# First mixer of a two-layer block: where modulation chunks 12 to 15 are summed, and when the scan's powers and between-states are made

## The reference, cut to what matters

```python
mod = sc @ ada_w[li] + ada_b[li]                       # 6 * 1024 columns a layer
sh1, sc1, g1, sh2, sc2, g2 = jnp.split(mod[:, None, :], 6, axis=-1)
...
p = softmax(q @ k.T * scale);  attn = p @ v            # first mixer, one half
states = s5_scan(ul, lam_bar, b_bar, ctx_final)        # s[t] = lam * s[t-1] + b u[t]
y = y + einsum('blgp,ghp->blgh', states, c_mat).real
z = gelu(y); s5 = z * sigmoid(z @ glu_w + glu_b)       # first mixer, other half
x = x + g1 * (concat([attn, s5]) @ w_out)
x = x + g2 * moe(modulate(rmsnorm(x), sh2, sc2), ...)
```

## Time and profile before

| what | value |
|---|---|
| median of 3 runs | 1443.02 us (1441.14 to 1443.29) |
| the profiled execution's own time | 1447.34 us |
| its span | 1445.5 us |
| busy: PE, DVE, ACT, POOL | 1303.6, 639.0, 300.4, 60.2 us |
| HBM | 347 GB/s over the span |
| granted TensorE clock, mean | 0.967 |

### The profile page before, as it was taken

The page is one execution under the profiler, slowest core; times in us unless marked ns, Lnnn a source line. Parts: engine busy times, 40 slices in busy tenths (PEclk is TensorE's granted clock), DMA queues, the critical chain, the costliest instruction groups (busy, mean ns, idle before and its releaser), DMA issues.

```text
span 1445.5 us, 21852 instructions
## 1 busy us (share of the span) xinstructions
PE 1303.6 (90%) x9044; PEld 678.7 (47%) x9044; DVE 639.0 (44%) x1175; ACT 300.4 (21%) x508; POOL 60.2 (4%) x112
## 2 busy tenths in 40 slices
PE   5999888999999978889888999999999978888888
PEld 1445335764444433334345676874454434333334
DVE  5998862254433222232233678864433323222232
ACT  2226342311111111111112113131111111111111
POOL 0000680000000000000000000000000000000000
PEclk9999999899999999999999999999999999999999
DMA  9673874959999999999998772587999999999995
GB/s 374 244 200 83 164 240 183 412 226 371 421 425 420 426 430 429 427 430 427 427 422 294 292 284 117 206 361 303 374 426 421 422 430 425 429 428 427 428 425 241
DMA packets 52598, 502.76 MB, mean 348 GB/s; under 512 B 9548, under 2 KB 16460, under 8 KB 20044
## 3 DMA queue, kind: packets, MB, share of 16 engines
q1 hardware_dynamic: 51948, 499.18, 86.0%
q10 hardware_dynamic: 544, 2.10, 0.4%
HBM read 496.57 MB, written 4.69 MB: 347 GB/s over the span
## 4 chain that ended last, share of the span: by engine, by line
PE 59%; DMA 28%; DVE 8%; issue 2%; SPq 1%; ACT 1%; DVEq 0%; ACTq 0%
PE ps L752 55%; DMA arena<-in_w_experts 23%; DMA arena<-in_ada_w 4%; PE ps L1070 2%; PE ps L446 2%; SPq L490 1%; DVE arena L2049 1%; ACT arena L1416 1%; DVE arena L2150 0%; DVE arena L1876 0%; PE ps L805 0%; DVE arena L1871 0%; DVE arena L1872 0%; DVE arena L1889 0%; PE ps L1017 0%
## 5 line engine op out<-in xcount | busy, mean ns | idle before, releaser
L752 PE MATMUL ps<-arena 128*32 128x512 f32 (+10 forms) x8224 | 1219.9, 485 | 122.0 <-issue 48.6
L752 PEld LDWEIGHTS ps<-arena 128*32 128x32 f32 (+5 forms) x8224 | 616.9, 130 | 709.9 <-issue 586.9
L1416 ACT ACTIVATE arena<-ps 128x512 f32<-128x512 f32 (+6 forms) x305 | 168.5, 552 | 926.2 <-PE ps L752 767.5
L1416 ACT ACTIVATE arena<-arena 128x256 f32<-128x256 f32 (+7 forms) x143 | 94.5, 682 | 153.2 <-DVE arena L2110 58.3
L2090 DVE SCALAR_TENSOR_TENSOR arena<-arena,ps 128x256 f32<-128x256 f32 x44 | 21.1, 480 | 233.7 <-ACT arena L1416 233.7
L2108 DVE CAST arena<-ps 128x512 bf16<-128x512 f32 x42 | 29.1, 692 | 165.2 <-PE ps L752 165.2
L2045 DVE COPY arena<-ps 128x512 f32<-128x512 f32 x44 | 30.4, 692 | 126.9 <-PE ps L752 126.9
L2078 DVE TENSOR_TENSOR arena<-arena 128x1024 bf16<-128x1024 f32 x42 | 51.5, 1225 | 37.3 <-ACT arena L1416 37.0
L1070 PE MATMUL ps<-arena 128*128 128x128 f32 x352 | 52.8, 273 | 0.0
L2110 DVE TENSOR_TENSOR arena<-ps,arena 128x1024 f32<-128x1024 f32 x42 | 51.4, 1224 | 1.4
L742 POOL MEMSET arena<- 128x1 f32 x2 | 0.2, 102 | 1192.3 <-PE ps L1070 1192.3
(11 more groups left out here) (234 smaller groups left out, 481.1 us busy)
## 6 DMA issues: line engine op xcount, KB each, us to landing
arena<-in_w_experts SPq DMA_DIRECT2D x76, 3072.0 KB, 20.8
arena<-in_w_experts SPq DMA_DIRECT2D x80, 1024.0 KB, 11.6
arena<-in_w_experts SPq DMA_DIRECT2D x38, 2048.0 KB, 19.8
arena<-in_ada_w SPq DMA_DIRECT2D x40, 1024.0 KB, 6.6
arena<-in_hy_w_in SPq DMA_DIRECT2D x6, 2048.0 KB, 11.1
arena<-in_ada_w SPq DMA_DIRECT2D x4, 2048.0 KB, 22.9
arena<-in_w_shared SPq DMA_DIRECT2D x2, 3072.0 KB, 10.1
arena<-in_hy_w_out SPq DMA_DIRECT2D x1, 4096.0 KB, 12.1
```

Of the source, the lines that this page charges most:

```text
L752: return pe.matmul(out, lhsT, rhs, start=start, stop=stop, skip_group_check=skip)
L1416: return act.activation(out, in_, func, **kw)
```

## The change

Four things are done.

1. On TensorE only chunk 11 stays in the softmax loop, now in step 2, ahead of that step's wait. Chunks 12 to 15 are summed on VectorE (`half_sum`, the body of `modulation_sum` made a function), four instructions a half. The first half of chunk 12 comes behind the softmax list and ahead of the last `attend_out`; then its second half, chunks 13 and 14, and the first half of chunk 15, all ahead of the wait for `y_mm`; the last half behind the eviction of y. TensorE folds the four sums with four products behind the gate products, and `ada_turn` goes behind part 7.
2. SP's list: chunk 12, the two attention loads, chunk 13, the wait for the last `attend`, `glu_w`, chunks 14 and 15, `w_s5`. The loads are as large as before and the buffer is the same; a half of the buffer now comes free when VectorE has summed it.
3. GpSimd squares all four powers when `qh_normed` is 1, into buffers of their own, and not between the levels of its tree.
4. The states between are made in iteration 14 of VectorE's softmax list, which there waits for `scan_done` 1.

```diff
-            for i in range(FILL_AT + 1, LATER - 1):
-                ada_load(i)
+            ada_load(FILL_AT + 1)
             load(w_att[0], A["ev_w_out"][:, 0:1], "wout_in")
             load(w_att[1], A["ev_w_out"][:, 1:4], "wout_in")
-            ada_load(LATER - 1)
+            ada_load(FILL_AT + 2)
             sp.wait_ge(sem("pv_mm"), HEADS // 2)
             sp.wait_ge(sem("wout_in"), 32)
             load(glu_w, A["glu_w"], "wout_in")
-            load(w_s5, A["ev_w_out"][:, 4:], "wout_in")
+            ada_load(FILL_AT + 3)
+            ada_load(LATER - 1)
+            load(w_s5, A["ev_w_out"][:, 4:], "w_s5_in")
...
+            pool.wait_ge(sem("qh_normed"), 1)
+            squared(pair_a, pair_b, A8, B8)
+            for n in range(3):
+                squared(*powers[n + 1], *powers[n])
             pool.wait_ge(sem("est_ready"), 8)
...
-                if n > 1:
-                    squared(step_a, step_b, a, b)
-                    a, b = step_a, step_b
...
             for n in range(2 * HEADS):
                 if n + 2 < 2 * HEADS:
                     scores(n + 2)
+                if n == 2:
+                    ada_chunk(pe, FILL_AT)
                 pe.wait_ge(sem("prob_ready"), n + 1)
...
-                if n % 3 == 0 and n > 0:
-                    ada_chunk(pe, FILL_AT + n // 3 - 1)
...
             attention_part(0)
-            ada_turn(pe, 0)
             attention_part(1)
...
+            pe.wait_ge(sem("ada_mm"), LATER)
+            for k in range(4):
+                a = 2 * (GROUP - 1 - (FILL_AT + 1 + k - FIRST))
+                last = pe.matmul(ps[32 * k:32 * k + 2 * GROUP, 7, :], first_pick[:, a:a + 2 * GROUP], first_sums[k], start=False, stop=k == 3, skip_group_check=True)
+            last.then_inc(sem("sums_mm"), 1)
             attention_part(7).then_inc(sem("att_mm"), 1)
+            ada_turn(pe, 0)
+            pe.wait_ge(sem("w_s5_in"), 16)
             pe.wait_ge(sem("s5_out"), 4)
...
             turned(act, f, ch, 2 * HEADS - 1)
-            ada_evict(act, f, ch, 0)
-            ada_copy(act, f, ch, 0)
...
+            ada_evict(act, f, ch, 0)
+            ada_copy(act, f, ch, 0)
...
+            def half_sum(i, half, out):
+
+                dve.wait_ge(sem(f"ada_in{half}"), 16 * (i - FIRST + 1))
+                for k in range(4):
+                    w, c = ada_half(i, half)[:, k], scz[:, 4 * half + k, 2 * GROUP - 2:2 * GROUP - 1]
+                    ins = ts(out, w, c, None, M) if half == 0 and k == 0 else stt(out, w, c, out, M, AD)
+                    if k < 3:
+                        ch(ins)
+                    elif half == 0:
+                        ins.then_inc(sem("ada_used"), 1)
+                        dve.wait_ge(sem("ada_used"), i - FIRST + 1)
+                    else:
+                        ins.then_inc(sem("ada_mm"), 1)
+                        dve.wait_ge(sem("ada_mm"), i + 1)
...
+                if n == 2 * HEADS - 2:
+                    dve.wait_ge(sem("scan_done"), 1)
+                    ch.then(pair_step(st[:, 3:2 + XCH:2], st[:, 2:2 + XCH:2], st[:, 2:2 + XCH:2, ::-1], est[:, XCH:NCH:2], XCH // 2), "combined")
                 if n >= 6 and n % 4 == 2:
                     attend_out(dve, ch, (n - 6) // 4)
...
+            half_sum(FILL_AT + 1, 0, first_sums[0])
             attend_out(dve, ch, HEADS // 2 - 1)
+            half_sum(FILL_AT + 1, 1, first_sums[0])
+            for half in range(2):
+                half_sum(FILL_AT + 2, half, first_sums[1])
+            for half in range(2):
+                half_sum(FILL_AT + 3, half, first_sums[2])
+            half_sum(FILL_AT + 4, 0, first_sums[3])
 
             dve.wait_ge(sem("y_mm"), 1)
             ch.then(dve.tensor_copy(ys.rearrange("p t (q b) c -> p b q t c", b=2)[:, 0],
                                     ps[:, 3, :].rearrange("p (q t c) -> p q t c", t=T5, c=C5)), "y_evicted")
+            half_sum(FILL_AT + 4, 1, first_sums[3])
```

More of the change, by code:

```diff
@@ L209, in program @@
         bm = at(rb, 4096).rearrange("p (b t r m) -> p b t r m", b=2, t=8, r=2)
-        step_a, step_b = (at(rb + 64 * i, 64).rearrange("p (r t) -> p r t", r=2) for i in (0, 1))
-        pair_a, pair_b = (at(rb + 64 * i, 64).rearrange("p (r t) -> p r t", r=2) for i in (2, 3))
-        tmp_a = at(rb + 256, 64).rearrange("p (r t) -> p r t", r=2)
+        powers = [[tiles(ri + 128 * i + 64 * j, 2, NT5) for j in (0, 1)] for i in range(4)]
+        pair_a, pair_b = powers[0]
+        tmp_a = tiles(ri + 512, 2, NT5)
         tree, pair_in, wide = (at(rb + 1024 * i, 1024).rearrange("p (s r t) -> p s r t", r=2, t=NT5) for i in (1, 2, 3))
@@ L421, in program @@
         row_pick = at(h3 + 18176, 4 * GROUP - 2)
+        first_sums = [at(rb + 1024 + ADC * k, ADC) for k in range(4)]
+        first_pick = at(rb, 4 * GROUP - 2)
         def short(c):
@@ L456, in ada_evict @@
         def ada_evict(act, f, ch, n):
-            act.wait_ge(sem("ada_mm"), (LATER, NADC)[n])
+            if n == 0:
+                act.wait_ge(sem("sums_mm"), 1)
+            else:
+                act.wait_ge(sem("ada_mm"), NADC)
             ch.then(f(adline[n], ps[:, 7, :], ACT.Copy), "adrow_ready")
@@ L706, in _ @@
             step(tree, a8, b8, est[:, 0:XCH:2], est[:, 0:XCH:2, ::-1], est[:, 1:XCH:2], wide, tree)
-            squared(pair_a, pair_b, A8, B8)
-            a, b, src, n = pair_a, pair_b, tree, 16
-            for out in (est[:, 0:8], tree[:, 0:4], est[:, 0:2], st[:, 2:3]):
+            src, n = tree, 16
+            for out, (a, b) in zip((est[:, 0:8], tree[:, 0:4], est[:, 0:2], st[:, 2:3]), powers):
                 n //= 2
@@ L1054, in _ @@
             pe.wait_ge(sem("z_ready"), 2)
-            pe.wait_ge(sem("wout_in"), 16 * 4)
+            pe.wait_ge(sem("wout_in"), 16 * 3)
             for j in range(4):
@@ L1907, in _ @@
                     ch(ins) if n == 2 else ch.then(ins, "combined")
+                if n == 2 * HEADS - 2:
+                    dve.wait_ge(sem("scan_done"), 1)
+                    ch.then(pair_step(st[:, 3:2 + XCH:2], st[:, 2:2 + XCH:2], st[:, 2:2 + XCH:2, ::-1], est[:, XCH:NCH:2], XCH // 2), "combined")
                 if n >= 6 and n % 4 == 2:
                     attend_out(dve, ch, (n - 6) // 4)
-            dve.wait_ge(sem("scan_done"), 1)
-            ch.then(pair_step(st[:, 3:2 + XCH:2], st[:, 2:2 + XCH:2], st[:, 2:2 + XCH:2, ::-1], est[:, XCH:NCH:2], XCH // 2), "combined")
+            ch(dve.memset(first_pick, 0.0))
+            ch(dve.memset(first_pick[:, 2 * GROUP - 2:2 * GROUP - 1], 1.0))
+            half_sum(FILL_AT + 1, 0, first_sums[0])
             attend_out(dve, ch, HEADS // 2 - 1)
+            half_sum(FILL_AT + 1, 1, first_sums[0])
[4 more added lines that the diff above has]
+            half_sum(FILL_AT + 4, 0, first_sums[3])
             dve.wait_ge(sem("y_mm"), 1)
@@ L2235, in modulation_sum @@
             def modulation_sum(n):
-                i = LATER + 2 * n
                 for half in range(2):
-                    dve.wait_ge(sem(f"ada_in{half}"), 16 * (i - FIRST + 1))
-                    for k in range(4):
-                        w, c = ada_half(i, half)[:, k], scz[:, 4 * half + k, 2 * GROUP - 2:2 * GROUP - 1]
-                        ins = ts(ada_sums[n], w, c, None, M) if half == 0 and k == 0 else stt(ada_sums[n], w, c, ada_sums[n], M, AD)
-                        if k < 3:
-                            ch(ins)
-                        elif half == 0:
-                            ins.then_inc(sem("ada_used"), 1)
-                            dve.wait_ge(sem("ada_used"), i - FIRST + 1)
-                        else:
-                            ins.then_inc(sem("ada_mm"), 1)
-                            dve.wait_ge(sem("ada_mm"), i + 1)
+                    half_sum(LATER + 2 * n, half, ada_sums[n])
             dve.wait_ge(sem("sc_ready"), 1)
```

1 line of the change is left out of this document (added).

## The result

The changed kernel takes 1448.35 us (median of 20 runs, 1444.18 to 1452.32), the kernel before 1443.03 us (20 runs): a ratio of 1.0029, 95% interval 1.0020 to 1.0037, so by the ratio 4.2 us slower (2.9 to 5.3; the two medians lie 5.3 apart). The forecast of "slower" and the range (1440.3 to 1450.0) hold, and 1446.1 us (+3.1) is near; of the terms behind that sum, several do not hold.

What follows compares the result with a forecast made beforehand. TensorE's products and the experts' weights were taken to bound the kernel, so only the first mixer's end counted. Terms 0.1 + 0.5 + 1.7 + 0.8 gave +3.1 us on 1443.02, 1446.1 us; range 1440.3 to 1450.0.

Steps and rivals of the forecast that it cites:

- Carrying one to one: End of the first mixer: whatever it loses or gains goes into the total one to one.
- Parts 1 and 2: Softmax loop and scan: chunk 11 costs nothing, two chunks leaving save 3.8 us; `scan_done` comes at 213.2, 6.2 earlier.
- the early squarings: nothing: GpSimd's squarings moved early, while VectorE reads mostly PSUM: no cost, at most their own 20 instructions of 0.3 us.
- Part 3: VectorE from iteration 14: stands for the scan until 213.3; `attend(3)` takes 2.85, its eviction done at 226.25, 3.2 us earlier.
- Part 4: VectorE's sums up to y: two loads in series at 5.1 us put y's eviction at 248.8, +0.1 us.
- rival B: Modulation loads take their middle 6.8 us: y evicted at 252.2, +3.4 on the sum, 1449.5 us; slower, chance 0.17.
- Part 5, fold, turn and clock: TensorE behind y: lower clock after idling +0.5 us, folding products and turn on the path +1.7.
- Part 5, the router's loads: Router's loads behind the experts' queue land 4.6 us later, needed 2.3 later: +0.8 us, between nothing and 2.
- small loads slip past: Lower bound at the router: its small loads are not held up by the queue, so their term is nothing.
- A: The sums keep pace: y evicted 4.3 to 8.9 earlier, total -1.6 to -6.2 us; faster, chance 0.25.
- C: Nothing reaches the end: router's loads slip past, clock does not fall, 1444.8 us; same, chance 0.12.

Runs made afterwards that it cites:

- f1: r6 with GpSimd's second tree level waiting until VectorE has done the rope's last 96x2048 product; ratio 0.9963 to the kernel before.
- e1: The changed kernel, but VectorE evicts y ahead of the first half of chunk 15, not behind it; ratio 1.0040 to the kernel before.
- e4: The changed kernel with a second buffer place for modulation chunks and `w_s5` loaded behind all sums; ratio 1.0032 to the kernel before.
- r0: The changed kernel with the router's three small loads issued ahead of expert 2; ratio 1.0032 to the kernel before.
- d8: The kernel before with eight unneeded products on TensorE behind part 7; ratio 1.0052, 7.5 us slower.
- r6: e4 with states between and last `attend_out` behind the softmax, ahead of all sums, and router's loads ahead of experts 1 and 2; 0.9949, 1435.8 us.
- rb: The kernel before with the router's loads issued ahead of expert 2, as control; ratio 0.9994.
- e3: The kernel before with only the early squarings on GpSimd and the states between in iteration 14, modulation chunks on TensorE; ratio 1.0007.

## Why the prediction came out right, point by point

The direction came out for the reason given, sums that wait for loads ahead of y. That +3.1 lies so near +4.2 is in good part luck. y was to be 0.1 late and was 5.2 late; fold, turn and clock came to 1.7 and not 2.2, the router's wait to 1.0 and not 0.8. Two things that the sum did not have took most of the excess back: the last 96 products took 1.16 less than in the trace of before, and the start of the second layer some 2.6 less (see "Carrying one to one").

**Parts 1 and 2 (right).** Chunk 11 cost nothing: it lies in a gap (181.00) that was there. The transposes of step 12 came at 209.62; counted from the softmax's start that is 34.3, against 36.9 before, so the two chunks won 2.6 of the 3.8. `scan_done` let VectorE go at 214.06, 0.8 after my 213.3.

**Part 2, "the early squarings: nothing" (failed step, +1.9 us on two products).** The squarings themselves were harmless, but taking them out of the tree brings GpSimd's 128x512 operations beside the rope's last two products, where the small squarings had stood. I had counted the moved instructions and not what moves up into their place. The second product took 3.24 to 3.26 us in every kernel with the early squarings except f1, and 2.29 in every one without them and in f1: 0.95 for certain, and in the changed kernel 0.9 more on the first one. The softmax starts 1.43 later and not 1.86, since the first product began 0.43 earlier in this trace (167.45 against 167.88). What this costs in the total is not shown: f1 takes it away and is no faster. Part 3 otherwise went as written: a wait of 2.84 in iteration 14 (4.6 predicted, since VectorE came later), the last scaling done at 222.09 (221.1), `attend(3)` in 3.68 us and not in 2.85. I had misread the latter as a time at half clock: it began at 226.08, behind the stretch at 0.50, and 226 to 230 was granted 0.76; in the changed kernel 224 to 228 was granted 0.52. Its eviction ended at 228.2, where I had 226.25.

**Part 4, "+0.1" (failed step: it measured +5.2).** The mechanism was the right one, loads in series in front of the eviction, but I had followed the wrong halves. By terms, the 5.1 between my 248.8 and the 253.90: 2.0 come from the late `attend(3)`; 0.35 from the wait for chunk 13's second half, whose load took 5.4; 0.65 more up to the end of chunk 14; and 2.1 from a third wait that I had not seen. I had let the first halves of chunks 14 and 15 be "landed meanwhile". But the load of 15's first half can be issued only when 14's first half has been summed, and that load took 8.5, not 5.1, with `glu_w` (1 MiB) issued 2.45 us before it on the same queue: landed at 242.8, summed at 245.7, and from there another 5.2 for the next. So the chain ran through the first halves, 8.5 + 5.2, and not through two second halves of 5.1 each. This is near rival B's price by another road: B had put y at 252.2. e1 and e4 show that the order and the places are the cause; no run has `glu_w` elsewhere. By an estimate from the same rows, with 5.4 for the load behind it too, y would have come at about 251.5.

The fit of the Trainium skill's page "DMA: Bandwidth & Descriptors", section "Anatomy of one DMA" (2.0 us plus bytes over 436 GB/s, an estimate of 4.4 for these loads), is for transfers issued by GpSimd and does not carry over to these: five loads of the changed kernel that had little in front of them took 5.0 to 5.8, and the one behind 1 MiB 8.5.

**Part 5, fold, turn and clock: +2.2 predicted, +1.70 measured.** The transposes of y behind 6.93 of idle took 1.97 where they took 1.03 before; at half the granted clock, as I had it from the earlier trace rows. The stretches of the changed kernel (columns as there):

```profile
250.00:254.00 4.00, 0.00 (x0) 0.00 (x0) 2.84 (x5) 0.00 (x0) 0.00 (x0) 0.72 1.03 363
254.00:258.00 4.00, 3.35 (x12) 3.09 (x13) 3.60 (x5) 1.26 (x2) 0.00 (x0) 0.50 1.02 434
```

TensorE idles in the first and is at 0.50, its lower level of 1.2 GHz, in the second. In e1, with 1.98 of idle, they took 1.09, and y to the last 96 was 14.99: so fold and turn are worth 0.7 on the path (1.6 from the start of the transposes to the last 96, 14.24 against 12.60, less the 0.9 by which the transposes follow y's eviction sooner, 0.75 against 1.66), and the clock about 1.0, where I had 1.7 and 0.5.

**Part 5, the router's loads: +0.8 (failed step).** In the changed kernel it was +1.03, near enough. But it was no small term: it is a second bound at almost the same height as the first, and I had given it 2 us at most. The case of my sum (y at 248.8) was nearly run: e1 has y at 248.12, and its router's products start 6.26 later than before, not 3.1. There the queue behind the modulation loads had not started at 246.0 but with `w_s5` at 248.48, since the last chunk's load came later; and `small loads slip past`, my lower bound, is refuted by 10.0 us for 256 KB. So one term was too low in each of two lanes that run side by side: what counts is the later of them, and each of the two holds the total at +4.6 to +5.8 us by itself (the mixer in r0, the queue in e1 and e4).

**Carrying one to one (right for a delay; for the change a term was missing).** d8's 5.9 us of delay gave 7.5 (5.3 to 9.8). Over all the kernels, the change of "router" and the change of time go together from -6.1 (r6: -7.4 us) to +6.1 (e1: +5.8 us), never more than some 2.7 apart. But the change also shortens a stretch far behind the mixer. From the router's products to the second layer's first products of 33x256 it takes 515.9 to 518.1 us in the four kernels that keep chunks 12 to 15 on TensorE (before, rb, d8, e3) and 513.2 to 515.0 in the ten that sum them on VectorE, in the mean 2.6 less. VectorE by time and TensorE by time at the start of the second layer, first in the kernel before, then in the changed one:

```profile
772.86 3.23 DVE L2150 SCALAR_TENSOR_TENSOR arena<-ps,arena 128x256 f32<-128x256 f32 x8 [5.89 <-issue]
798.79 1.06 PE L446 MATMUL ps<-arena 128*24 128x512 f32 x8 [1.88 <-DMA arena<-in_ada_w]
801.21 1.80 PE L446 MATMUL ps<-arena 128*24 128x512 f32 x8 [1.36 <-DMA arena<-in_ada_w]
```

```profile
774.66 3.46 DVE L2187 SCALAR_TENSOR_TENSOR arena<-ps,arena 128x256 f32<-128x256 f32 x8 [1.99 <-PE ps L758]
803.19 2.11 PE L448 MATMUL ps<-arena 128*24 128x512 f32 x16
```

In the four, VectorE idles 5.7 to 6.5 us without a releaser ahead of adding the expert mixture to x (L2150), and TensorE then waits 1.3 to 3.2 us in all for the modulation weights of the second layer; in the ten, VectorE idles 1.99 for TensorE and the weights cost 0 to 0.8. SP issues these weights only when x is done, so they come sooner there. Why VectorE stands in the four stays open, and no run takes this effect out by itself. As an estimate, the 6.8 us by which the router's products are late, less these 2.6, are the 4.2 of the total; r6's 7.4 may owe as much to it.

**Rivals.** A (faster) needed y before 245.8; r6 has it at 242.37 and is faster by 0.51%, so the mechanism exists, with the waits taken away. B (loads at their middle time) did not come as written: five of the six loads took 5.0 to 5.8. C fell with the same measurement as the slip.

## What to carry to other kernels

Work moved from the bound engine to an idle one is only free if its data can be there: a buffer of one place makes every sum pay a whole load, and each such sum in front of another eviction hands that wait on. When two lanes end within a few us of each other (here y and the queue in front of the router's loads), mending one can show nothing, and a null result for it is no evidence against it: mend both before judging. And when instructions are taken out of an engine's list, price what moves up into their place, not only what left.

## What the runs showed of the hardware

**VectorE and GpSimd take turns on products read from SBUF.** GpSimd by time in the changed kernel, beside the two VectorE products above:

```profile
167.32 1.29 POOL L706 TENSOR_TENSOR arena<-arena 128x512 f32<-128x512 f32 x1
168.70 3.19 POOL L707 TENSOR_TENSOR arena<-arena 128x512 f32<-128x512 f32 x1
171.97 3.20 POOL L708 TENSOR_TENSOR arena<-arena 128x512 f32<-128x512 f32 x1
```

VectorE's first product starts at 167.45, while GpSimd's runs until 168.61: 168.61 + 2.29 = 170.90 (measured end 170.77). GpSimd's next, from 168.70, ends 1.29 behind that, 172.06 (171.89); VectorE's second 2.29 behind that, 174.18 (174.04); GpSimd's third at 175.33 (175.17). In these four each engine's instruction runs for its full time alone while the other waits. The Trainium skill's page "SBUF — State Buffer", section "Who interferes with whom", says that a VectorE instruction with two SBUF inputs contends with a GpSimd instruction that reads SBUF, and that contention for the port pair that the two share is an exclusive lock. The trace agrees, within 0.17 us at each of the four ends.

**A load of 194.5 KB waits for what stands in front of it on its queue.** `in_mcst` landed in 4.6 us before, 5.8 in the changed kernel and 12.1 in e1, where it was issued 6.75 us earlier behind the same experts; the moments of landing, 291.55 and 291.1, are nearly one.
